# Half of the state-space angle tables made inside the second expert loop, in a buffer outside the weight ring

## The reference, cut to what matters

```python
dt = jnp.exp(log_dt)[:, None]
mag, ang = jnp.exp(a_re * dt), a_im * dt
lb_re, lb_im = mag * jnp.cos(ang), mag * jnp.sin(ang)
...
# s[t] = lb * s[t-1] + bu[t], complex, over 256 tokens, for 32 groups x 64 states
_, _, s_re, s_im = lax.associative_scan(combine, (ar, ai, bu_re, bu_im), axis=1)
y = jnp.einsum('blgp,gcp->blgc', s_re, c_re) - jnp.einsum('blgp,gcp->blgc', s_im, c_im)
```

## Time and profile before

| What | us |
|---|---|
| three executions | 1986.45, 1987.51, 1988.85; median 1987.51 |
| profiled execution, its own time | 1985.39 |
| its span | 1983.6 |
| TensorE busy | 1761.0 (89%) |
| VectorE busy | 1048.9 (53%) |
| GpSimd busy | 563.6 (28%) |
| ScalarE busy | 417.1 (21%) |
| mean granted TensorE clock | 0.955 of full speed |

### The profile page before, as it was taken

The page is one execution under the profiler, slowest core; times in us unless marked ns, Lnnn a source line. Parts: engine busy times, 40 slices in busy tenths (PEclk is TensorE's granted clock), DMA queues, the critical chain, the costliest instruction groups (busy, mean ns, idle before and its releaser), DMA issues.

```text
span 1983.6 us, 56204 instructions
## 1 busy us (share of the span) xinstructions
PE 1761.0 (89%) x23585; PEld 1216.2 (61%) x23586; DVE 1048.9 (53%) x2460; ACT 417.1 (21%) x834; POOL 563.6 (28%) x423
## 2 busy tenths in 40 slices
PE   6999989999999997998989966666668999999998
PEld 4544456666666664645766744444446676788887
DVE  3898167766676767756355633333248996210001
ACT  2001252111122114115342211111113224110001
POOL 0000027766677762001024422222239000100000
PEclk9999989999999997999999988888888999999999
DMA  9854178999999999914379999999996352233320
GB/s 366 326 206 169 43 275 349 430 429 429 409 429 413 428 428 394 351 48 155 128 311 415 426 429 429 429 429 429 429 414 218 128 212 85 85 128 128 131 103 21
DMA packets 109376, 574.28 MB, mean 290 GB/s; under 512 B 4976, under 2 KB 10224, under 8 KB 84592
## 3 DMA queue, kind: packets, MB, share of 16 engines
q1 hardware_dynamic: 108720, 570.72, 71.9%
q10 hardware_dynamic: 576, 2.43, 0.3%
HBM read 572.08 MB, written 1.05 MB: 289 GB/s over the span
## 4 chain that ended last, share of the span: by engine, by line
PE 62%; DMA 25%; DVE 7%; issue 2%; ACT 2%; SPq 2%; DVEq 0%; ACTq 0%
PE bank L367 25%; PE bank L581 14%; DMA ring<-in_expert_w_gate 13%; DMA ring<-in_expert_w_down 7%; PE bank L553 4%; PE bank L1040 4%; DMA ring<-in_expert_w_up 4%; PE bank L531 3%; DVE b L1100 2%; PE bank L628 2%; ACT b L1934 2%; PE bank L438 1%; PE bank L960 1%; DMA ring<-in_conv_w_in 1%; SPq L2436 1%
## 5 line engine op out<-in xcount | busy, mean ns | idle before, releaser
L581 PE MATMUL bank<-ring,b 128*32 128x128 f32 (+1 forms) x13600 | 518.2, 309 | 133.1 <-DMA ring<-in_expert_w_gate 70.7
L581 PEld LDWEIGHTS bank<-ring,b 128*32 128x32 f32 x13600 | 400.8, 115 | 305.2 <-issue 154.1
L1100 DVE TENSOR_TENSOR h_t<-h_t,bank 128x512 f32<-128x512 f32 (+1 forms) x696 | 349.4, 562 | 306.9 <-PE bank L553 306.9
L367 PE MATMUL bank<-h_t,ring 128*128 128x256 f32 (+1 forms) x1600 | 425.6, 428 | 8.3 <-ACT h_t L1934 5.8
L1934 ACT ACTIVATE b<-bank 128x256 f32<-128x256 f32 (+4 forms) x370 | 142.2, 402 | 1243.1 <-PE bank L581 741.5
L367 PEld LDWEIGHTS bank<-h_t,ring 128*128 128x128 f32 x1600 | 307.4, 193 | 119.9 <-issue 80.1
L2380 POOL TENSOR_SCALAR b<-b 128x1024 f32<-128x1024 f32 (+1 forms) x85 | 195.1, 2295 | 55.4 <-POOL b L2388 33.6
L2388 POOL TENSOR_TENSOR b<-b 128x512 f32<-128x512 f32 (+1 forms) x85 | 88.8, 1045 | 405.4 <-PE bank L553 405.3
L553 PE MATMUL bank<-b 32*128 32x512 f32 (+1 forms) x1392 | 169.7, 558 | 5.7 <-DVE h_t L1100 4.8
L1100 DVE TENSOR_TENSOR b<-b,bank 128x128 f32<-128x128 f32 (+3 forms) x124 | 49.9, 406 | 235.1 <-PE bank L367 157.4
L2383 POOL TENSOR_TENSOR b<-b,b 128x1024 f32<-128x1024 f32 (+1 forms) x85 | 161.4, 1899 | 7.1
(11 more groups left out here) (316 smaller groups left out, 1451.8 us busy)
## 6 DMA issues: line engine op xcount, KB each, us to landing
ring<-in_expert_w_gate SPq DMA_DIRECT2D x64, 2048.0 KB, 18.4
ring<-in_expert_w_up SPq DMA_DIRECT2D x64, 2048.0 KB, 20.6
ring<-in_expert_w_down SPq DMA_DIRECT2D x64, 2048.0 KB, 20.8
ring<-in_ada_w SPq DMA_DIRECT2D x24, 2048.0 KB, 14.1
...
```

The source lines that it names most:

```text
L367: last = pe.matmul(o, lhs(k), rhs(k), start=(k == 0), stop=(k == nk - 1))
L581: last = pe.matmul(b[32 * m:32 * m + 32, 0:width], lhs[:, k, :], rhs[:, k, m * width:(m + 1) * width], start=(k == 0), stop=(k == nk - 1), ...
L1100: return dv.tensor_tensor(o, a, b, op)
```

## The change

Phases 0 and 1 move. Their tables no longer lie in the ring but in `b12` (columns 2048 to 6144), which is unused in the second expert loop, and GpSimd makes their angles inside that loop: the first ten chunks are written out, and after each of them comes one of the five steps of a phase (`phase_part`). ScalarE takes their sines right after its own loop, before it loads the table for the square root. Phases 2 and 3 are made after the loop as before, in one ring slot instead of two, and the wait for the second slot goes. As a slot less is left empty (one `None` instead of two in a row), every later load moves up in the list: pieces 28 to 30 and the chunks of `w_in_2` by one to three places. The squares of the norms ln3 and rms1 move to `b12` columns 6144 to 8192. On TensorE misc now comes ahead of `state_inputs(2)`; on ScalarE the sines of phase 2 come where those of phase 1 were, and those of phase 3 keep their place behind misc.

```diff
@@ -109,8 +109,7 @@
     attn = iter([part[2]] + part[:2] + part[3:] + cols(w["attn_w_out"][0], [0, 512, 1024]))
     middle = [next(attn) if p is None else pieces[p] for p in MIDDLE]
     w_in = cols(w["w_in_2"][0], [0, 512, 1024, 1476, 1988, 2500, 3012, 3524])
-    nothing = [None] * 2
-    after = nothing + pieces[28:31] + w_in[:1] + nothing + w_in[1:5] + nothing + w_in[5:]
+    after = [None] + pieces[28:31] + w_in[:2] + [None] + w_in[2:] + [None]
     after += cols(w["w_ssm_glu_2"][0], [0, 1024, 2048])
     after += cols(w["w_attn_proj_2"][0], [0, 1024]) + cols(w["w_out_2"][0], [0, 512, 1024])
     edges = list(range(0, FFN, 512)) + [FFN]
@@ -214,8 +213,11 @@
             if p < 18:
                 return conv_chunk(5) + 2 + p - 12
             if p in CHAIN:
-                return start["after"] + 2 + p - 28
+                return start["after"] + 1 + p - 28
             return start["middle"] + MIDDLE.index(p)
+
+        def w_in_chunk(j):
+            return start["after"] + 4 + j + (j > 1)
 
         attn_chunk = [start["middle"] + j for j, p in enumerate(MIDDLE) if p is None]
 
@@ -247,6 +249,7 @@
 
         second_sum = [b12[:, 4352 + 512 * i:4864 + 512 * i] for i in range(3)]
         squares, cln_sq = v3(b12, 4096, KD, TOK), v3(b3, 0, 4, TOK)
+        late_squares = v3(b12, 6144, KD, SEQ)
         mean4, std4, inv4 = [b3[:, 4352 + P * i:4352 + P * (i + 1)] for i in range(3)]
         eps = {"ln": sm[:, 24:25], "cln": sm[:, 24:25], "rms": sm[:, 25:26]}
 
@@ -295,8 +298,9 @@
         def s5w(i):
             return X[:, i // 2, SEQ + P * (i % 2):SEQ + P * (i % 2) + P]
 
-        phase_slots = [(start["after"] + j) % RING for j in range(2)]
-        phases = [[v3(ring, phase_slots[i // 2] * SLOT + 2048 * (i % 2) + 1024 * j, 4, SEQ) for j in range(2)] for i in range(4)]
+        phase_slot = start["after"] % RING * SLOT
+        phases = [[v3(b12, 2048 + 2048 * i + 1024 * j, 4, SEQ) for j in range(2)] for i in range(2)]
+        phases += [[v3(ring, phase_slot + 2048 * i + 1024 * j, 4, SEQ) for j in range(2)] for i in range(2)]
         turned = [v4(b3, 0, 4, 2, SEQ), v4(h_t, 2048, 4, 2, SEQ)]
         turning = v4(b3, 2048, 4, 2, SEQ)
         gelu_t, wuk_t = b3[:, 5632:5888], v3(b3, 5120, 4, P)
@@ -430,7 +434,8 @@
 
                 norm_sum(f"ln{i}", "ready", ones_d[:, :], [X[:, k, 0:ntok] for k in range(KD)])
                 spread_mean(f"ln{i}", ntok)
-                norm_sum(f"ln{i}", "squared", ones_d[:, :], [squares[:, k, 0:ntok] for k in range(KD)])
+                sq = late_squares if i == 3 else squares
+                norm_sum(f"ln{i}", "squared", ones_d[:, :], [sq[:, k, 0:ntok] for k in range(KD)])
                 spread_inverse(f"ln{i}", ntok)
 
             def transposes(b, pieces):
@@ -870,13 +875,13 @@
             norm_sums(3, SEQ)
             piece(30)
             turn_piece(28)
-            norm_sum("rms1", "squared", ones_d[:, :], [squares[:, k, 0:SEQ] for k in range(KD)])
+            norm_sum("rms1", "squared", ones_d[:, :], [late_squares[:, k, :] for k in range(KD)])
             piece(29)
             turn_piece(30)
             spread_inverse("rms1", SEQ)
             turn_piece(29)
             mark("chain_pieces")
-            n = start["after"] + 5
+            n = w_in_chunk(0)
             pe.wait_ge(a_free, lane["a"])
             mark("states_in")
             def state_inputs(i):
@@ -902,7 +907,7 @@
                 mark(f"read_out{i}")
 
             def in_projection(j):
-                channel_out(n + 2 + j + 2 * (j > 4), "a", lambda k: U[:, k, :], KD, 512, SEQ)
+                channel_out(w_in_chunk(j), "a", lambda k: U[:, k, :], KD, 512, SEQ)
 
             loaded(n)
             w_states = chunk(n, KD, 512)
@@ -917,9 +922,9 @@
             state_inputs(1)
             in_projection(1)
             read_out(0)
+            token_out(w_in_chunk(2), "a", lambda k, t: U[:, k, t * P:(t + 1) * P], 2, 452)
+            mark("misc")
             state_inputs(2)
-            token_out(n + 4, "a", lambda k, t: U[:, k, t * P:(t + 1) * P], 2, 452)
-            mark("misc")
             read_out(1)
             in_projection(3)
             state_inputs(3)
@@ -945,13 +950,12 @@
             pe.wait_ge(a_free, marks["dsa_turned"][1])
             index(0)
             index(1)
-            in_projection_last = n + 15
-            channel_out(in_projection_last, "a", lambda k: U[:, k, :], KD, 512, SEQ)
+            in_projection(6)
 
             def glu(j, m):
                 if m == 0:
-                    loaded(n + 16 + j)
-                wt = chunk(n + 16 + j, 4, 1024)
+                    loaded(n + 13 + j)
+                wt = chunk(n + 13 + j, 4, 1024)
 
                 def emit(b):
                     for k in range(4):
@@ -962,7 +966,7 @@
                     return last
                 group("a", emit)
                 if m == KD - 1:
-                    done_with(n + 16 + j)
+                    done_with(n + 13 + j)
                 mark(f"glu{j}")
 
             def latent_query(h):
@@ -1017,8 +1021,8 @@
             latent_out(7)
             mark("values")
             pe.wait_ge(a_free, marks["values"][1])
-            channel_out(n + 18, "v", lambda k: atto[:, k, :], 4, 1024, SEQ)
-            n += 9
+            channel_out(n + 15, "v", lambda k: atto[:, k, :], 4, 1024, SEQ)
+            n += 6
             pe.wait_ge(sem("merged"), 1)
             pe.wait_ge(a_free, lane["a"])
             for j in range(2):
@@ -1975,7 +1979,7 @@
                 take_mean(ntok)
                 if between:
                     between()
-                square(f"ln{i}", X[:, :, 0:ntok], KD, squares, f"ln{i}_centred")
+                square(f"ln{i}", X[:, :, 0:ntok], KD, late_squares if i == 3 else squares, f"ln{i}_centred")
                 root(f"ln{i}", ntok)
 
             def modulate_scaled(norm, i, part, event):
@@ -2005,6 +2009,12 @@
                         ins = act(o[:, m, src * SEQ:(src + 1) * SEQ], b[:, src * SEQ:(src + 1) * SEQ], ACT.Copy,
                                   scale=mod(i, part, m, src))
                     taken(ins)
+
+            def phase(i):
+                cos_t, sin_t = phases[i]
+                ac.wait_ge(sem("phase_ready"), i + 1)
+                act(sin_t, sin_t, ACT.Sin, scale=TWO_PI).then_inc(sem("phase_done"), 1)
+                act(cos_t, cos_t, ACT.Sin, scale=TWO_PI).then_inc(sem("phase_done"), 1)
 
             def moe(layer, tiles, pieces=((), (), ())):
                 ntok = tiles * P
@@ -2058,6 +2068,9 @@
                     act(silu_g, bank[0][:, 0:P], ACT.Silu).then_inc(s["gate_taken"], 1)
                     ac.wait_ge(s["y_full"], n + 1)
                     act(y_sb, bank[2][:, 0:256], ACT.Copy).then_inc(s["y_taken"], 1)
+                if layer == 1:
+                    for i in range(2):
+                        phase(i)
                 fetch_root()
                 if layer == 0:
                     ac.wait_ge(sem("moe_done0"), 1)
@@ -2220,7 +2233,7 @@
             norm_stats(3, SEQ)
             for k in range(KD):
                 scaled("ln3", k, KD)
-                act(squares[:, k, 0:SEQ], X2[:, k, :], ACT.Square, scale=pr("ln2_g", 8 + k, 1), bias=pr("ln2_b", 8 + k, 1)) \
+                act(late_squares[:, k, :], X2[:, k, :], ACT.Square, scale=pr("ln2_g", 8 + k, 1), bias=pr("ln2_b", 8 + k, 1)) \
                     .then_inc(sem("rms1_squared"), 1)
             take_piece(30)
             take_turned(28)
@@ -2248,26 +2261,18 @@
                     b = full()
                     taken(act(dst[:, m, :], b[:, 0:SEQ], ACT.Sigmoid))
 
-            def phase(i):
-                cos_t, sin_t = phases[i]
-                ac.wait_ge(sem("phase_ready"), i + 1)
-                act(sin_t, sin_t, ACT.Sin, scale=TWO_PI).then_inc(sem("phase_done"), 1)
-                act(cos_t, cos_t, ACT.Sin, scale=TWO_PI).then_inc(sem("phase_done"), 1)
-
             def gelu_tanh(i):
                 ac.wait_ge(sem("gelu_arg"), i + 1)
                 act(gelu_t, gelu_t, ACT.Tanh, scale=GELU_C).then_inc(sem("gelu_tanh"), 1)
 
             given_to_vector(1)
-            phase(0)
             ac.wait_ge(a_free, taken.n)
             for m in range(1, 4):
                 b = full()
                 taken(act(xs_t[:, m, :], b[:, 0:SEQ], ACT.Copy))
-            phase(1)
+            phase(2)
             take_query_projection()
             take_read_out(0)
-            phase(2)
             take_misc()
             phase(3)
             ac.wait_ge(sem("kv_stats"), 1)
@@ -2363,6 +2368,23 @@
                     po.tensor_scalar(X[:, k, 0:ntok], X[:, k, 0:ntok], pr(f"{name}_g", 8 * j + k, 1),
                                      pr(f"{name}_b", 8 * j + k, 1), ALU.mult, ALU.add).then_inc(sem(f"x_normed{i}"), 1)
 
+            def phase_part(i, part):
+
+                cos_t, sin_t = phases[i]
+                if part == 0:
+                    it = cn("iota").unsqueeze(1).broadcast_to([P, 4, SEQ])
```

(40 more changed lines are left out.)

## The result

| | kernel before | changed kernel |
|---|---|---|
| median of five executions each, first comparison | 1987.51 (1986.45 to 1995.55) | 1976.73 (1973.58 to 1983.35) |
| ratio, 95% interval | | 0.9938 (0.9923 to 0.9952) |
| second comparison (`after_again` below) | 1989.89 | 1978.62, ratio 0.9946 (0.9932 to 0.9960) |
| third comparison (`after_third` below) | 1988.73 | 1978.65, ratio 0.9948 (0.9933 to 0.9962) |
| profiled execution, first comparison; its span | 1985.39; 1983.6 | 1983.35; 1981.3 |

The change is a gain. On the median of before, the first ratio is 12.3 us (9.5 to 15.3), the second 10.7 and the third 10.3; forecast were 8.4. Over the three comparisons the mean of 17 executions of the changed kernel is 1978.2 us and that of 39 of the kernel before 1989.3, so 11.1 us, with about 1.6 either way by their spread.

The account below looks back on a forecast made before the run. It took the S5 part as bound by VectorE's scans, held up by GpSimd, then narrowly TensorE, and the loop by weight loads. Gains of 8.1 and 9.0 us met at 8.4, other terms nothing: 1987.51 - 8.4 = 1979.1 us, range 1976.3 to 1983.7.

Parts of the forecast that it names:

- Part 1: VectorE's first run_states: with GpSimd idle, its adds, scans and large multiplications run as in the third call, saving 8.42 us.
- Part 2: TensorE up to read_out(1): no wait for scans, no state_inputs(2) stall, misc at full clock in the new order, 7.87 us.
- Part 3: Projection at 1614.32 us, where VectorE's 9.0 us and TensorE's 8.1 us gains meet: 8.4 us taken, nearer to TensorE.
- Part 4: End of ScalarE's loop: four sines and a table load delay the next load 5.3 us, hidden in 7.02 us idle.
- Part 5: Second expert loop: GpSimd's ten added steps priced at nothing, as loads hide them; bounds 0 and 13.4 us.
- Part 6: Weight ring: loading one slot more ahead gains nothing; competing with the last down weights costs at most 4.9 us.
- (a): S5 part: clock does not hold, misc stays at 14.17 us, gain about 6.7, 1980.8 us; chance 0.20.
- (b): First run_states is slow for another reason; only the new order's 2.72 us counts, 1984.8 us; chance 0.06.
- (c): End of the loop: piece 28 takes 4.9 us from the last down weights, gain 3.5, 1984.0 us; chance 0.06.
- (d): Expert loop: GpSimd's steps hold VectorE and TensorE, DMA queue runs dry, 5.0 us slower, 1992.5 us; chance 0.05.
- (e): Tables of phases 0 and 1 late, or GpSimd still working after 1505 us: no gain, 1987.5 us; chance 0.05.

Follow-up runs that it names:

- after_again: The changed kernel measured once more with nothing edited: 1978.62 us, ratio 0.9946 to the kernel before.
- after_third: The changed kernel measured again, unedited, with a profile: 1978.65 us, ratio 0.9948 to the kernel before.
- one_input: The kernel before with GpSimd's six two-input steps of phases 2 and 3 replaced by one-input ones, those tables left out: 1980.32 us, ratio 0.9953.
- old_order: The changed kernel with state_inputs(2) ahead of misc again: 1983.26 us, ratio 0.9959 to the kernel before.
- no_loop_steps: The changed kernel without GpSimd's ten angle steps in the expert loop, two tables left out, ScalarE's sines kept: 1976.92 us, ratio 0.9924 to the kernel before.
- ring_as_before: The changed kernel with the weight list of before, two empty slots in a row: 1977.96 us, ratio 0.9938 to the kernel before.
- order_only: The kernel before with one edit, misc ahead of state_inputs(2): 1988.28 us, ratio 0.9992 to the kernel before.
- before_clear: The kernel before with the sums of the first expert loop cleared by ScalarE, not GpSimd: 1990.05 us, ratio 0.9998 to the kernel before.

## Why the prediction came out as it did

The direction, the place and the main mechanism were right; the forecast gain of 8.4 us was too small. In the first comparison (12.3 us) it was short by 3.9. Of these, 0.7 lie in the stage that the change touches, and the step behind them is known (part 3). The rest no stage shows: over the 56 executions of all three comparisons about 2 us are left outside the stage, and their cause stays open.

**Part 1** (-8.42 on VectorE): exact, 2.36 + 4.76 + 4.49. Its premise, that two-input instructions alone do it, was wrong for 1.6 us of the 5.29 (`one_input`); the sum did not suffer, since it was taken from the third call.

**Part 2** (-7.87 on TensorE): right in sum. From the start of the S5 stretch, the projection after `read_out(1)` began 49.57 us later in before and 41.54 in the changed kernel, 8.03. But the reason was half wrong: the forecast put the stall of `state_inputs(2)` and the slow misc down to the order, and with the old order they are gone as well (`old_order`).

**Part 3** is the step that failed: "I take 8.4 us, nearer to TensorE". Up to 1593 us TensorE has gained those 8.03, but the projection at 1614.32 waits 1.38 us for ScalarE, which waits for VectorE, before and after alike; so VectorE's gain of 9.0 is what reaches it. From the last add of the loop the projection comes 139.96 us later in before and 130.91 in the changed kernel, 9.05 us: the upper end of the 8.1 to 9.0, and not the lower. The wait was in the earlier trace rows and should have decided it. The same part says that what follows "moves as a whole": the rest was 369.3 to 369.5 us before and 366.7 to 370.9 in the changed kernel, so no profile shows that term to be nothing, and none its size.

**Part 4** (sines free): right.

```profile
1484.36 3.88 ACT L1938 ACTIVATE b<-b 128x1024 f32<-128x1024 f32 x4
1488.26 1.28 ACT L1938 ACT_TABLE_LOAD   x1
...
1492.99 0.28 ACT L1938 ACTIVATE b<-bank 128x128 f32<-128x128 f32 x1 [3.24 <-PE bank L633]
```

Of the 7.02 us of idle in the earlier trace rows, 3.24 are left, and the norm stage is no longer in that profile (38.91 and 38.99).

**Part 5** (loop at nothing): right in the profiles, 449.13 and 449.23 us in the first two; by the executions a cost of some 2 us is not excluded (`no_loop_steps`). The gain was not gone, as the loop is bound by its DMA (share 0.99 and 1.01 in the rows above). The rule of the Trainium skill, "GPSIMD Engine Reference", section "Key points", names VectorE instructions with two SBUF inputs. The trace agrees with it in the tail (scans of 2.27 and 2.79 us instead of 0.66) and in the loop, though the two rows that the forecast set side by side are from two chunks: GpSimd's add beside the one of 128x4 elements at 1070.01 began at 1069.98 us. The same section names VectorE instructions in a two-port mode too. That may bear on the norm stage, where a one-input row takes 5.81 us beside GpSimd and 2.67 without; no run here shows the mode.

**Part 6** (ring at nothing): right (`ring_as_before`).

**Rivals.** (a) fell: misc 12.40 at a clock of 1.00. (b) fell: `one_input` has the buffers of before and a first call with adds at 2.36, scans at 7.16 and multiplications at 4.49; and the new order alone (`order_only`) gave 0.3 us of stretch and not the 2.7 of (b). (c) and (d) fell with the loop's length. (e) fell with GpSimd's last row: it is silent 15.5 us ahead of the first scan.

**The sum.** The changed kernel's medians are 1976.73, 1978.62 and 1978.65 us against a forecast of 1979.1. A gain of 8.4 us would be a ratio of 0.9958; the intervals of the second and third comparison reach it, that of the first (up to 0.9952) does not. Of the 11.1 us over all executions, 9.1 are the S5 stretch. For the other 2.0 (with their 1.6 either way) the four profiles of each kernel have, as means, 39.1 and 37.8 us in the norm stage, 369.35 and 368.9 in the rest, and 448.0 and 448.7 in the loop, so 1.1 us of gain in stages where the single values overlap. Ahead of the loop they have 1028.8 and 1030.6, a loss of 1.8 in code that is the same; so the mean spans of the eight profiles differ by 8.4 us, and that this is the forecast is luck. In the norm stage it is the clock again: in `after_again`, which has the 36.11, the 16 matmuls ahead of the S5 stretch take 3.69 us at a granted clock of 1.00, where the first profile of the changed kernel has 6.37 at 0.57. Short norm stages came with the old S5 part as well, 38.05 us in `order_only` and 37.76 in `before_clear`. The forecast priced this stage at nothing, between -0.5 and +0.5. Whether the change moves these stages or the executions at hand did is not settled.
